# First layer of a three-layer block: new column order, convolution, normalisation and attention run beside later columns

## The chip, the cores and the metric

The kernel runs on one core of a Trainium2 chip, in one launch. The metric is the device time of that launch in microseconds, from first to last instruction with what lies around them. Five engines matter: TensorE (PE in the profile; its weight loads are listed apart as PEld), VectorE (DVE), ScalarE (ACT), GpSimd (POOL) and SyncE (SP), which issues nearly all DMAs. PSUM has eight banks of 512 fp32 columns: four are `lin_ps`, four are `ps`.

## The reference

256 tokens with 2048 features pass through three layers. Only the first is rebuilt:

```python
z = rmsnorm(x) @ w_in                                  # [256, 2048] @ [2048, 7168]
a_val, a_gt, a_gate, q, k, v, b_gate = split(z, 7 x 1024)
u  = (a_val + b0) * sigmoid(a_gt + b1)
y  = causal_depthwise_conv(u, w_dw, 31 taps) + b_dw    # per channel, along the tokens
y  = silu(layernorm(y) * ln_g + ln_b)                  # over the 1024 channels
ya = (y @ w_pw + b_pw) * silu(a_gate)
yb = causal_attention(q, k, v, 8 heads of 128) * silu(b_gate)
x  = x + concat(ya, yb) @ w_out
```

With 256 tokens the block-sparse attention of the reference is plain causal attention. The second layer is a latent attention with an indexer, the third a gated DeltaNet with a Fourier branch and an MLP of 8192; each ends with a projection that is added to `x`.

## The kernel before

**Products in two parts.** Every fp32 weight is split on the chip: ACT rounds a tile to fp32r (`w_hi`, helper `hi`), POOL subtracts (`w_lo`, L543), and the activations are kept as such a pair as well (`a` and `b`, `[P, 16, 2, 256]`, feature chunks by high or low part by tokens). Weights come in *units* of 128x1024 (512 KB, one DMA), through four slots of `raw`, `w_hi` and `w_lo`. The order of the units is fixed by hand (`LINEARS`), and each engine counts them: `raw_in`, `hi_done`, `lo_done`, `unit_used`. ACT may split unit u once unit u - 4 is used up. In the text, unit numbers are those of this order: 0 to 111 are `w_in`, 112 to 119 the pointwise matrix `w_pw`, 120 to 151 `w_out`.

**Two kinds of units.** A *product* unit (`product`) has weights stationary, 4 chunks of features and 256 output columns. For each chunk and each of two column halves it issues one matmul of 512 columns (the high weights on both parts of the activations, L1889) and one of 256 (the low weights on the high part, L1891): 8 pairs. Four units make a *group*, whose result has features on partitions; one DVE reduction adds its two parts and moves it into `z` (`group_free` counts these evictions, L1130, L1175, L1199). A *wide* unit (`outer_unit`, L1929 to L1931) has activations stationary and 512 output columns moving: 12 matmuls of 512, with tokens on partitions in the result. `w_out` uses wide units. A group may start when the group two before it is evicted.

**The first layer, in order.** TensorE runs groups 0 to 23 in a row, in the order of the columns of `w_in`. ACT takes the sigmoid of two channel chunks at a time (L694), and DVE runs the convolution in four rounds of two chunks, 58 tap instructions each (L1202), beside groups 8 to 23. Then come, on TensorE:

1. the channel sum over partitions with a matrix of ones (L1947), group 24, and the sum of squares in the same way (L1953);
2. groups 25 to 27, during which DVE and ACT finish the normalisation in the layout with features on partitions;
3. the eight units of `w_pw`; after each group DVE adds the parts (L1240), the bias and the gate (L1244), and splits the result (L1248, L1250);
4. the attention, in a loop of four rounds of two heads with nothing else between its steps: transpose of v (L1967), scores (L1970), mask, maximum, exp, scale, transposes of the probabilities (L1977), product with v (L1982), gate and split (L1284, L1286);
5. `w_out` (32 wide units).

The second layer's attention has rounds of two heads too, but with product units between the steps: scores (L2129), some units, transposes (L2137), some units, product with v (L2146), with ACT's exp at L811 and its scaling at L817. Most of its rounds have the causal upper part left out: 128 + 256 columns of scores instead of 2 x 256.

Of the kernel before, what the change touches and what calls it, by code (L numbers as in the profile page):

```python
# [17 lines left out]
F32 = mybir.dt.float32  # L18
# [7 lines left out]
P = 128  # L26
# [58 lines left out]
GROUPS = (("even_w_in", 28), ("even_w_pw", 4), ("even_w_out", 4), ("odd", 38), ("odd_w_out", 4), ("w_in_2", 20),  # L85
# [79 lines left out]
for _ph in range(4):  # L165
    OUTS[f"mlp{_ph}"] = (UNIT0["mlp"] + 64 * _ph + 32, GROUP0["mlp"] + 12 * _ph + 8)
PLAIN = ("even_w_out", "w_o_2", "mlp0", "mlp1", "mlp2")
# [6 lines left out]
def build(nc, t, out):  # L174
    ctx = ExitStack()
    with ctx:
# [11 lines left out]
        def rounds(name, names):  # L188
# [81 lines left out]
        ln_act = steps("ln_act", [f"sq{s}" for s in range(4)] + ["root"] + [y for s in range(4) for y in (f"silu{s}a", f"silu{s}b")]  # L270
                       + [f"hi{s}" for s in range(4)] + ["agate", "bgate"])
        ln_pe = steps("ln_pe", ["mean"] + [f"var{s}" for s in range(4)])
        ln_dve = steps("ln_dve", [f"c{s}" for s in range(4)] + ["rstd"] + [f"n{s}" for s in range(4)] + [f"lo{s}" for s in range(4)])

        at_pe = [steps(f"at_pe{w}", ["vt", "s", "pt", "o"]) for w in range(2)]
        at_dve = [rounds(f"at_dve{w}", ["vtok", "mask", "max", "neg", "rsum", "n0", "n1", "ptc", "o", "hi", "lo"]) for w in range(2)]
        at_act = [steps(f"at_act{w}", ["qs", "vs", "p0", "p1"]) for w in range(2)]
        pw_dve = steps("pw_dve", ["g0", "g1", "hi", "lo"])
# [44 lines left out]
        e_q, e_v, e_vt = ([z[:, 8 * w + n, :] for w in range(2)] for n in range(3))  # L323
        e_s, e_pt = ([z[:, 8 * w + n:8 * w + n + 2, :] for w in range(2)] for n in (3, 5))
# [12 lines left out]
        addm = dmask[:].rearrange("p a b -> p (a b)")[:, 0:3 * P]  # L337
        o_flat = [v.rearrange("p a b -> p (a b)") for v in o_s]
# [69 lines left out]
        def _(sp):  # L408
# [24 lines left out]
            def stream_out(name, u0, row0=0):  # L433

                v = t[name].rearrange("(k p) n -> p k n", p=P)
                with sp.Fori(0, NB) as i:
                    col = sp.snap(i * BLK)
                    for j in range(8):
                        slot = (u0 + j) % SLOTS
                        sp.wait_ge(lo_done, i * 8 + (u0 + j - SLOTS + 1))  # L440
                        sp.dma_start(raw[:, slot].rearrange("p (k n) -> p k n", k=2),
                                     v[:, row0 + 2 * j:row0 + 2 * j + 2, bass.ds(col, BLK)]).then_inc(raw_in[slot], 16)
# [9 lines left out]
            for q in range(4):  # L452
                load(4 + q, q, first[:, q * UK:(q + 1) * UK, UN:2 * UN])
# [6 lines left out]
            stream("even_w_in", 8, 26, 4, col0=2 * UN)  # L460
# [7 lines left out]

            def free_slot(u):
                sp.wait_ge(lo_done, u - SLOTS + 1)  # L470
                return u % SLOTS
# [87 lines left out]
        def _(act):  # L559
# [122 lines left out]
            his(8, 24)  # L682

            with act.Fori(0, 4) as i:
                for n in range(16):
                    slot = n % SLOTS
                    act.wait_ge(raw_in[slot], i * 64 + 16 * ((32 + n) // SLOTS + 1))
                    act.wait_ge(unit_used, i * 16 + (32 + n - SLOTS + 1))
                    nc.scalar.activation(w_hi[:, slot], raw[:, slot], ACT.Copy).then_inc(hi_done, 1)  # L689
                    if n == 3:  # L690
                        act.wait_ge(group_free, 8)
                        for y in range(2):
# [3 lines left out]
            for n in range(4):  # L696
                hi(96 + n, n)
# [1743 lines left out]
```

## Time and profile before

| | us |
|---|---|
| median of 3 runs | 2332.21 |
| lowest, highest | 2326.82, 2333.15 |
| the profiled execution | 2328.57 |
| its span, first to last instruction | 2326.8 |
| PE busy | 2245.7 (97%) |
| POOL busy | 1727.3 (74%) |
| DVE busy | 1025.9 (44%) |
| ACT busy | 1049.6 (45%) |

Times inside the execution count from the start of its span. A PE matmul's own duration is longer than the distance to the next, because they are pipelined: the pace is read from the distances of starts, or from a stretch divided by its count. "PEclk" is the granted clock of TensorE as a share of full speed.

### The profile page before, as it was taken

What the parts mean: (1) busy time and instruction counts of PE and PEld (TensorE: products, weight loads), DVE (VectorE), ACT (ScalarE), POOL (GpSimd) and SP (SyncE); (2) the same over time, 40 slices, a digit from 0 to 9 for tenths busy, and PEclk for the clock granted to TensorE, in tenths of its full rate; (3) what the DMA queues carried; (4) which work ended last, traced back from release to release, by engine and by line L of the source; (5) the groups of instructions that cost most, each with busy time, mean ns of one, the idle gap of its engine ahead of it and who ended that gap; (6) DMA issues with size and microseconds to landing.
All of it is one profiled execution on the core that took longest, in us unless ns stands there. A gap on an engine that the chain in (4) does not pass through costs nothing.

```text
span 2326.8 us, 35399 instructions
## 1 busy us (share of the span) xinstructions
PE 2245.7 (97%) x12194; PEld 1925.9 (83%) x12194; DVE 1025.9 (44%) x1798; ACT 1049.6 (45%) x1442; POOL 1727.3 (74%) x723
## 2 busy tenths in 40 slices
PE   7999996899999999999999999999999999999998
PEld 6888885778888778888888888887888888888886
DVE  2176647212765133365656553503831631731731
ACT  5444453345457554445353535445333333333343
POOL 6888873478756876565565657887888888888886
PEclk9999998899999999999999999999999999999999
DMA  6666652355545655454444534565666666666654
GB/s 212 189 190 189 189 156 80 98 183 148 162 127 154 215 163 154 127 154 114 140 130 125 145 109 162 183 212 157 190 190 191 188 190 192 187 189 191 188 189 146
DMA packets 325519, 383.86 MB, mean 165 GB/s; under 512 B 14654, under 2 KB 263333, under 8 KB 325157
## 3 DMA queue, kind: packets, MB, share of 16 engines
q1 hardware_dynamic: 321333, 376.75, 54.0%
q10 hardware_dynamic: 4080, 5.64, 0.8%
q8 instruction: 74, 1.21, 0.2%
q14 instruction: 32, 0.26, 0.0%
HBM read 380.24 MB, written 2.10 MB: 164 GB/s over the span
## 4 chain that ended last, share of the span: by engine, by line
PE 92%; DVE 3%; issue 1%; ACT 1%; POOL 1%; DMA 1%; ACTq 0%; DVEq 0%; POOLq 0%; SPq 0%
PE lin_ps L1889 37%; PE lin_ps L1891 18%; PE lin_ps L1929 8%; PE lin_ps L1931 8%; PE lin_ps L1930 8%; PE ps L2295 1%; PE ps L1860 1%; POOL w_lo L543 1%; PE ps L2288 1%; PE ps L2294 1%; PE ps L2214 1%; DVE scr L1244 1%; DMA raw<-in_odd_w_out 0%; PE ps L2146 0%; PE lin_ps L2008 0%
## 5 line engine op out<-in xcount | busy, mean ns | idle before, releaser
L543 POOL TENSOR_TENSOR w_lo<-raw,w_hi 128x1024 fp32r<-128x1024 f32 x716 | 1726.9, 2421 | 580.8 <-ACT w_hi L571 450.5
L1889 PE MATMUL lin_ps<-a,w_hi 128*128 128x512 f32 x3328 | 1184.1, 400 | 0.4 <-POOL w_lo L543 0.4
L1891 PE MATMUL lin_ps<-a,w_lo 128*128 128x256 f32 x3328 | 929.5, 279 | 0.0
L1889 PEld LDWEIGHTS lin_ps<-a,w_hi 128*128 128x128 f32 x3328 | 626.0, 188 | 149.7 <-issue 2.9
L1891 PEld LDWEIGHTS lin_ps<-a,w_lo 128*128 128x128 f32 x3328 | 628.1, 189 | 2.6 <-issue 1.9
L571 ACT ACTIVATE w_hi<-raw 128x1024 fp32r<-128x1024 f32 x360 | 378.8, 1060 | 452.4 <-PE lin_ps L1891 257.2
L582 ACT ACTIVATE w_hi<-raw 128x1024 fp32r<-128x1024 f32 x260 | 276.3, 1063 | 442.4 <-PE lin_ps L1891 283.2
L1929 PE MATMUL lin_ps<-w_hi,b 128*128 128x512 f32 x768 | 300.1, 391 | 2.1 <-POOL w_lo L543 1.9
L1931 PE MATMUL lin_ps<-w_hi,b 128*128 128x512 f32 x768 | 298.8, 389 | 0.0
L1930 PE MATMUL lin_ps<-w_lo,b 128*128 128x512 f32 x768 | 298.8, 389 | 0.0
L1929 PEld LDWEIGHTS lin_ps<-w_hi,b 128*128 128x128 f32 x768 | 144.3, 188 | 33.4 <-POOL w_lo L543 3.5
L1931 PEld LDWEIGHTS lin_ps<-w_hi,b 128*128 128x128 f32 x768 | 144.2, 188 | 30.0
L1930 PEld LDWEIGHTS lin_ps<-w_lo,b 128*128 128x128 f32 x768 | 144.3, 188 | 29.8
L1889 PE MATMUL lin_ps<-b,w_hi 128*128 128x512 f32 x416 | 147.8, 399 | 5.8 <-DVE scr L1240 3.1
L1147 DVE SCALAR_TENSOR_TENSOR x<-x,lin_ps 128x512 f32<-128x512 f32 x32 | 20.6, 684 | 297.2 <-PE lin_ps L1931 297.2
L1891 PE MATMUL lin_ps<-b,w_lo 128*128 128x256 f32 x416 | 116.5, 280 | 0.0
L689 ACT ACTIVATE w_hi<-raw 128x1024 fp32r<-128x1024 f32 x64 | 67.9, 1061 | 95.3 <-PE lin_ps L1891 95.3
L1889 PEld LDWEIGHTS lin_ps<-b,w_hi 128*128 128x128 f32 x416 | 78.1, 188 | 26.3 <-DVE scr L1240 3.4
L1202 DVE SCALAR_TENSOR_TENSOR ps<-z,vec,ps 128x254 f32<-128x254 f32 (+28 forms) x232 | 88.9, 466 | 0.1
L1821 DVE TENSOR_REDUCE scr<-lin_ps 128x512 f32<-128x1024 f32 x32 | 39.2, 1225 | 112.4 <-PE lin_ps L1891 112.4
L1823 DVE SCALAR_TENSOR_TENSOR scr<-scr 128x512 f32<-128x512 f32 x32 | 86.5, 2704 | 1.1
L1825 DVE CAST b<-scr 128x512 f32 x32 | 78.8, 2464 | 5.1 <-DVE scr L1823 5.1
(379 smaller groups left out, 2135.5 us busy)
## 6 DMA issues: line engine op xcount, KB each, us to landing
raw<-in_w_in SPq DMA_DIRECT2D x144, 512.0 KB, 3.7
raw<-in_w_mlp_up SPq DMA_DIRECT2D x128, 512.0 KB, 3.8
raw<-in_w_mlp_down SPq DMA_DIRECT2D x128, 512.0 KB, 4.7
raw<-in_even_w_in SPq DMA_DIRECT2D x112, 512.0 KB, 3.6
raw<-in_odd_w_in SPq DMA_DIRECT2D x40, 512.0 KB, 3.7
raw<-in_even_w_out SPq DMA_DIRECT2D x32, 512.0 KB, 3.6
raw<-in_odd_w_out SPq DMA_DIRECT2D x32, 512.0 KB, 4.6
raw<-in_w_o SPq DMA_DIRECT2D x32, 512.0 KB, 4.8
```

Of the source, the lines that this page charges most:

```text
L543: nc.gpsimd.tensor_tensor(w_lo[:, slot], raw[:, slot], w_hi[:, slot].bitcast(F32), ALU.subtract).then_inc(lo_done, 1)
L571: nc.scalar.activation(w_hi[:, slot], raw[:, slot], ACT.Copy).then_inc(hi_done, 1)
L582: nc.scalar.activation(w_hi[:, slot], raw[:, slot], ACT.Copy).then_inc(hi_done, 1)
L689: nc.scalar.activation(w_hi[:, slot], raw[:, slot], ACT.Copy).then_inc(hi_done, 1)
L1202: nc.vector.scalar_tensor_tensor(out=acc[c][:, :, k:T], in0=u[c][:, :, 0:T - k], scalar=per_channel(w + 8 * (TAPS - 1 - k) + c), in1=acc[c ...
L1823: nc.vector.scalar_tensor_tensor(out=tm2, in0=tmp, scalar=0.0, in1=tmp, op0=ALU.max, op1=ALU.mult).then_inc(ml_dve.sem, 1)
L1825: nc.vector.tensor_copy(bb[:, :, 0, :], tm2).then_inc(ml_dve.sem, 1)
L1889: nc.tensor.matmul(acc, hi[:, k, m * P:(m + 1) * P], src[:, kk].rearrange("p s n -> p (s n)"), start=(q == 0 and k == 0), stop=False)
L1891: last = nc.tensor.matmul(acc[:, 0:T], lo[:, k, m * P:(m + 1) * P], src[:, kk, 0, :], start=False, stop=(q == n - 1 and k == UK - 1))
L1929: nc.tensor.matmul(acc, ah, hi[:, k, :], start=(kk == 0), stop=False)
L1930: nc.tensor.matmul(acc, ah, lo[:, k, :], start=False, stop=False)
L1931: last = nc.tensor.matmul(acc, al, hi[:, k, :], start=False, stop=(kk == DC - 1))
```

## The change

1. **Column order.** `w_in` is read as the list `EVEN` says: value and sigmoid gate of the convolution alternate (groups 0 to 7), then q, k (8 to 15), v (two wide groups, 16 and 17), the attention's gate (18 to 21), the convolution's gate (22 to 25). 28 groups become 26; the number of units stays 112.
2. **Convolution.** Its four rounds are unrolled and start once their own two groups are there; the evictions of groups 2 to 11 are placed between the taps.
3. **Values.** v is computed with tokens on partitions (wide units), so no head's v is transposed.
4. **Normalisation.** The convolution's result is turned onto tokens (16 transposes of 128x128), DVE takes mean and variance with `bn_stats` and `bn_aggr`, scales, and 16 transposes turn it back between wide units 4 and 5 of group 17. ACT applies silu in PSUM. The products with ones are gone.
5. **Attention.** Its four rounds run between units 96 and 115: scores before unit 96, 101, 106, 111, transposes two units later, product with v four units later. The upper triangle is left out as in the second layer; ACT scales the probabilities and rounds the output.
6. **Pointwise units.** For each weight half three matmuls of 256 columns (high-high, high-low, low-high) into the same columns, so no reduction follows; the bias and gate are applied in PSUM, ACT rounds into `a`, DVE subtracts.
7. **`w_out`** starts with the attention's half (`FROM`), then takes the pointwise half from `a`. SP's loop for it and for the other wide projections is unrolled.
8. **All product units of the kernel:** `product` issues high, high, low, low instead of high, low, high, low.

```diff
+EVEN = []
+for _n in range(4):
+    EVEN += [(Z_AVAL + 2 * _n, _n * UN), (Z_AGT + 2 * _n, CW + _n * UN)]
+EVEN += [(Z_Q + 2 * _n, 3 * CW + _n * UN) for _n in range(4)]
+EVEN += [(Z_K + 2 * _n, 4 * CW + _n * UN) for _n in range(4)]
+EVEN += [(Z_V + 4 * _n, 5 * CW + _n * 512) for _n in range(2)]
+EVEN += [(Z_BGATE + 2 * _n, 6 * CW + _n * UN) for _n in range(4)]
+EVEN += [(Z_AGATE + 2 * _n, 2 * CW + _n * UN) for _n in range(4)]
+E_ROUNDS = (96, 101, 106, 111)
...
 # ScalarE
+            for last, i in ((11, 0), (22, 1), (31, 2), (42, 3)):
+                his_up(8 if i == 0 else (12, 23, 32)[i - 1], last)
+                gates(i)
+            his_up(43, 74)
+            preload(1)
+            his_up(75, 77)
+            act.wait_ge(ln_dve.sem, ln_dve.at("ag1"))
+            nc.scalar.activation(bn_root, ..., ACT.Sqrt, bias=eps[:, 0:1]).then_inc(ln_act.sem, 1)
+            his_up(78, 80)
+            act.wait_ge(ln_pe.sem, ln_pe.at("t2"))
+            for c in range(8):                     # silu in PSUM; unit 81 after the fourth
...
+            for r, first in enumerate(E_ROUNDS):
+                his_up(done_to + 1, first + 2)
+                if r == 0:
+                    act.wait_ge(group_free, 22)
+                    gate = z[:, Z_BGATE:Z_BGATE + 8, :]
+                    nc.scalar.activation(gate, gate, ACT.Silu).then_inc(ev_act.sem, 1)
...                                                # exp, scale, two units, (r == 3: silu of a_gate), one unit
 # VectorE
+            taken = ({12: 2, 24: 3}, {5: 4, 17: 5, 28: 6}, {8: 7, 20: 8, 30: 9}, {10: 10, 22: 11})
...
+            for g in range(12, 17):
+                even_out(g)
...                                                # bn_stats x4, bn_aggr x2, reciprocal, scale x4, masks
+            for r in range(4):
+                both(e_scores, r)
+                if r == 3:
+                    even_out(25)
+                both(e_sums, r)
+                both(e_turned, r)
+                if r in (1, 2):
+                    even_out(22 + r)
+                if r == 3:
+                    pw_gate(0)
+                both(e_out, r)
...
 # TensorE, product
                     for m in range(2):
-                        acc = lin_ps[:, 2 * parity + m, :]
-                        nc.tensor.matmul(acc, hi[:, k, m * P:(m + 1) * P], src[:, kk].rearrange("p s n -> p (s n)"),
-                                         start=(q == 0 and k == 0), stop=False)
-                        last = nc.tensor.matmul(acc[:, 0:T], lo[:, k, m * P:(m + 1) * P], src[:, kk, 0, :],
+                        nc.tensor.matmul(lin_ps[:, 2 * parity + m, :], hi[:, k, m * P:(m + 1) * P],
+                                         src[:, kk].rearrange("p s n -> p (s n)"), start=(q == 0 and k == 0), stop=False)
+                    for m in range(2):
+                        last = nc.tensor.matmul(lin_ps[:, 2 * parity + m, 0:T], lo[:, k, m * P:(m + 1) * P], src[:, kk, 0, :],
                                                 start=False, stop=(q == n - 1 and k == UK - 1))
 # TensorE, first layer
+            for g in range(16):
+                for q in range(4):
+                    product(4 * g + q, g, g % 2, q, 4, q, a, 0, in_ready if g == 0 else None, g >= 2)
+            for j in range(8):
+                wide_unit(E_VAL + j, 16, j, of_a, j)
...                                                # 16 transposes
+            for j in range(8):
+                if j == 5:
+                    pe.wait_ge(ln_dve.sem, ln_dve.at("n11"))
...                                                # 16 transposes back
+                wide_unit(E_VAL + 8 + j, 17, j, of_a, j)
...
+            for u in range(E_REST, PW + 8):
+                for r, first in enumerate(E_ROUNDS):
+                    if u == first:
+                        e_scores(r)
+                    if u == first + 2:
+                        e_turned(r)
+                    if u == first + 4:
+                        e_outputs(r)
+                if u < PW:
+                    g = 18 + (u - E_REST) // 4
+                    product(u, g, g % 2, u % 4, 4, u % 4, a, 0, None, True)
+                else:
+                    pw_unit(*divmod(u - PW, 2))
```

## Rows read from the trace of the kernel before

**Rows 1.** The page: busy time of the engines, and its two costliest groups.

```profile
PE 2245.7 (97%) x12194; PEld 1925.9 (83%) x12194; DVE 1025.9 (44%) x1798; ACT 1049.6 (45%) x1442; POOL 1727.3 (74%) x723
...
L543 POOL TENSOR_TENSOR w_lo<-raw,w_hi 128x1024 fp32r<-128x1024 f32 x716 | 1726.9, 2421 | 580.8 <-ACT w_hi L571 450.5
L1889 PE MATMUL lin_ps<-a,w_hi 128*128 128x512 f32 x3328 | 1184.1, 400 | 0.4 <-POOL w_lo L543 0.4
```

**Rows 2.** Windows of the first layer: stretch, its length, busy time per engine, clock, DMA.

```profile
28.70:289.60 260.90, 260.90 (x1508) 228.20 (x1506) 125.50 (x285) 114.62 (x114) 227.05 (x95) 1.00 0.63 191
289.60:308.60 19.00, 18.32 (x98) 15.38 (x96) 7.16 (x12) 8.68 (x10) 12.75 (x6) 1.00 0.50 152
...
358.80:370.90 12.10, 5.82 (x32) 4.84 (x32) 11.66 (x10) 5.20 (x7) 8.13 (x4) 0.99 0.44 139
370.90:428.70 57.80, 36.28 (x113) 26.82 (x114) 38.80 (x92) 18.66 (x51) 0.37 (x1) 0.65 0.05 15
428.70:515.90 87.20, 87.17 (x385) 71.83 (x383) 6.23 (x11) 36.63 (x43) 73.36 (x31) 1.00 0.57 176
```

**Rows 3.** Waits of PE from 358 to 428.7: total, times, longest.

```profile
PE ps L1977 <- DVE z L1270: 13.1, 4, 5.4
PE ps L1967 <- ACT z L740: 11.1, 4, 3.2
PE lin_ps L1889 <- DVE scr L1240: 3.1, 1, 3.1
```

**Rows 4.** Lines of PE, 28.7 to 289.4: count, busy time, mean ns.

```profile
L1889 PE MATMUL lin_ps<-a,w_hi 128*128 128x512 f32 x752 | 260.8, 394 | 0.0
```

**Rows 5.** The same for a stretch of the MLP, 2138.2 to 2222.

```profile
L1889 PE MATMUL lin_ps<-a,w_hi 128*128 128x512 f32 x238 | 84.1, 399 | 0.0
```

**Rows 6.** Timelines: start, length, instruction. A pair and the next, then eight small matmuls.

```profile
150.11 0.39 PE L1889 MATMUL lin_ps<-a,w_hi 128*128 128x512 f32 x1
150.34 0.27 PE L1891 MATMUL lin_ps<-a,w_lo 128*128 128x256 f32 x1
150.46 0.40 PE L1889 MATMUL lin_ps<-a,w_hi 128*128 128x512 f32 x1
...
1049.78 1.06 PE L2295 MATMUL ps<-z 128*128 128x128 f32 x8
```

**Rows 7.** Timeline of TensorE in one attention round of the second layer.

```profile
720.55 1.47 PE L2129 MATMUL ps<-z 128*128 128x128 f32 x8
721.67 0.58 PE L1889 MATMUL lin_ps<-a,w_hi 128*128 128x512 f32 x1
...
727.50 0.82 PE L2137 MATMUL ps<-ident,z 128*128 128x128 f32 x6
728.08 0.48 PE L1889 MATMUL lin_ps<-a,w_hi 128*128 128x512 f32 x1
...
730.94 1.47 PE L2146 MATMUL ps<-z 128*128 128x256 f32 x8
732.17 0.47 PE L1889 MATMUL lin_ps<-a,w_hi 128*128 128x512 f32 x1
```

**Rows 8.** DVE and ACT in that round.

```profile
720.75 1.23 DVE L1296 TENSOR_REDUCE z<-lin_ps 128x512 f32<-128x1024 f32 x1 [1.47 <-PE lin_ps L1891]
...
723.39 0.41 ACT L811 ACTIVATE z<-z,stat 128x128 f32<-128x128 f32 x1 [3.63 <-DVE stat L1434]
...
725.68 1.49 ACT L817 ACTIVATE z<-z,stat 128x128 f32<-128x128 f32 x4
```

**Rows 9.** Lines of DVE in one convolution round, 160.3 to 204.6.

```profile
L1202 DVE SCALAR_TENSOR_TENSOR ps<-z,vec,ps 128x254 f32<-128x254 f32 (+28 forms) x58 | 22.2, 467 | 0.0
```

**Rows 10.** Lines of ACT, 305 to 357.

```profile
L731 ACT ACTIVATE z<-z 128x2048 f32<-128x2048 f32 x1 | 1.9, 1902 | 0.0
L709 ACT ACT_TABLE_LOAD x1 | 1.3, 1283 | 0.0
```

**Rows 11.** Lines of DVE, 505 to 600: nearest to the new scaling from PSUM.

```profile
L1334 DVE TENSOR_SCALAR scr<-lin_ps,stat 128x512 f32<-128x512 f32 x2 | 1.4, 746 | 0.0
```

More of the change, by code:

```diff
@@ L727, in _, with his_up @@
-            for n in range(4):
-                hi(108 + n, n)
-            his(UNIT0["even_w_pw"], 8)
-            act.wait_ge(group_free, 28)
-            nc.scalar.activation(z[:, Z_BGATE:Z_BGATE + 8, :], z[:, Z_BGATE:Z_BGATE + 8, :],
-                                 ACT.Silu).then_inc(ln_act.sem, 1)
-            ahead(UNIT0["even_w_out"])
-            act.wait_ge(ln_dve.sem, ln_dve.at("lo3"))
-            with act.Fori(0, HE // 2) as i:
+            def his_up(first, last):
+                for u in range(first, last + 1):
+                    hi(u, u % SLOTS)
@@ new lines, in _, with pointwise @@
+                his_up(first + 5, first + 5)
+                done_to = first + 5
+                def pointwise(g):
+                    bank = 2 * ((PW_G + g) % 2)
+                    act.wait_ge(pw_dve.sem, pw_dve.at("g1", g))
+                    nc.scalar.activation(a[:, 2 * g:2 * g + 2, 0, :], lin_ps[:, bank:bank + 2, 0:T], ACT.Copy).then_inc(pw_act.sem, 1)
+                if r == 3:
+                    pointwise(0)
+                for w in range(2):
+                    act.wait_ge(at_dve[w].sem, at_dve[w].at("gate", r))
+                    nc.scalar.activation(b[:, 8 + 2 * r + w, 0, :], ps[:, 2 * w, 0:T], ACT.Copy).then_inc(at_act[w].sem, 1)
@@ L1225, in _ @@
-            even_out(25)
+            for g in range(12, 17):
+                even_out(g)
+            for q in range(TT):
+                for h in range(2):
+                    dve.wait_ge(ln_pe.sem, ln_pe.at("t1"))
+                    nc.vector.bn_stats(bn[:, 12 * q + 6 * h:12 * q + 6 * h + 6], ps[:, 2 * q + h, :]).then_inc(ln_dve.sem, 1)
+            for q in range(TT):
+                dve.wait_ge(ln_dve.sem, ln_dve.at(f"bn{q}1"))
+                nc.vector.bn_aggr(bn_two[:, 2 * q:2 * q + 2], bn[:, 12 * q:12 * q + 12]).then_inc(ln_dve.sem, 1)
@@ L1287, in _ @@
+            for g in range(1, 4):
+                pw_gate(g)
+                pw_low(g)
             to_x("even_w_out", 1)
@@ L1942, in _ @@
             vectors(0, 1, 2)
[L1943 removed]
+            in_ready = normed(0)
             pe.wait_ge(bld, 3)
[L1945 to L1955 removed]
@@ new lines, in pw_unit @@
+            def pw_unit(g, q):
+                u, bank = PW + 2 * g + q, 2 * ((PW_G + g) % 2)
+                if q == 0:
+                    pe.wait_ge(group_free, PW_G + g - 1)
+                pe.wait_ge(lo_done, u + 1)
+                hi = w_hi[:, u % SLOTS].rearrange("p (k n) -> p k n", k=UK)
+                lo = w_lo[:, u % SLOTS].rearrange("p (k n) -> p k n", k=UK)
+                for k in range(UK):
+                    kk = UK * q + k
+                    for m in range(2):
+                        acc, cols = lin_ps[:, bank + m, 0:T], slice(m * P, (m + 1) * P)
+                        nc.tensor.matmul(acc, hi[:, k, cols], b[:, kk, 0, :], start=(kk == 0), stop=False)
+                        nc.tensor.matmul(acc, hi[:, k, cols], b[:, kk, 1, :], start=False, stop=False)
+                        last = nc.tensor.matmul(acc, lo[:, k, cols], b[:, kk, 0, :], start=False, stop=(kk == 2 * UK - 1))
+                last.then_inc(unit_used, 1)
```

438 lines of the change are left out of this document (211 added, 227 removed).

## Prediction, made before the changed kernel was run

> **What bounds the kernel now.** I read the page first: PE is busy 2245.7 us of the span, POOL 1727.3 us [rows 1]. PE sets the time nearly everywhere, and POOL is next: a unit costs it 2.42 us, while PE takes 8 pairs of matmuls for one. So any gain must come from PE: idle time, extra instructions, or its pace.
>
> The windows of the first layer come second [rows 2]. From 28.7 to 289.6 PE is full: 752 pairs in 260.8 us [rows 4], 0.347 us each, 2.77 us a unit. The wide units of `w_out` go at 87.2 us / 385 = 0.2265 us a matmul, 2.72 us a unit [rows 2]. Between them lie 139 us that look different. From 370.9 to 428.7 stands the attention alone: 57.8 us, PE busy 36.3, POOL 0.4, and the granted clock at 0.65 on average, that is, much of it at the 1.2 GHz level, after idle gaps [rows 2].
>
> The waits name the gaps: 13.1 us for the scaled probabilities, 11.1 us for the copies of v, 3.1 us for the pointwise stage's split [rows 3]. DVE, ACT and POOL do nothing for other work meanwhile. The question is what is left of these 139 us when the attention lies between product units.
>
> **What goes away.**
> - Windows 289.6 to 308.6: 19.0 us hold one group (32 x 0.347 = 11.1); the rest, 7.9 us, is the two products with ones and one wait for the convolution [rows 2, 4].
> - 358.8 to 370.9: 12.1 us hold two pointwise units (5.5); 6.6 us are waits for the pointwise results [rows 2].
> - 370.9 to 428.7: all 57.8 us [rows 2].
> Together 72.3 us.
>
> **What comes.**
> - Attention beside units. The second layer's round has the same shapes. Its scores hold PE from 720.55 to 721.67, its transposes from 727.50 to 728.08, its outputs from 730.94 to 732.17: 1.12 + 0.58 + 1.23 = 2.93 us [rows 7]. Four rounds: 11.7 us.
> - 32 transposes of 128x128. Eight fp32 matmuls of that size take 1.06 us from first start to last end, 0.78 without the last one's length, 0.11 each [rows 6]: 3.6 us.
> - v as two wide groups: 16 x 2.72 instead of 16 x 2.77: -0.8 us.
> - Pointwise units: 24 matmuls of 256 columns instead of 8 pairs. A pair costs 0.347 and a wide matmul 0.2265 [rows 2, 4], so the 256 columns cost 0.120; 24 x 0.120 = 2.88 instead of 2.77, eight times: +0.9 us.
>
> **What the cover leaves open.** Between scores and transposes two units run. In the second layer that was just enough: ACT's last scaling ended at 725.68 + 1.49 = 727.17, and PE came to it at 727.50 [rows 7, 8], although an eviction of 1.23 us stood before DVE's mask [rows 8]. The rounds of the new code are the same, with more room later (two units before the outputs), but two are not:
> - Round 0: ACT must first wait for the eviction of group 21, then take silu of the whole `b_gate` (1.9 us) and load the table for exp (1.28 us) [rows 10]. The eviction ends 1.3 us after the scores begin; silu ends at 3.2, the table is there at 4.5. The second layer's exp started 2.84 us after its scores [rows 7, 8]. So everything is 1.7 us later, 0.33 of which was spare: I take a stall of 1.5 us, with 0 and 3 as the ends.
> - Round 3: `even_out(25)` stands before the sums on DVE; unit 111 ends 1.12 + 2.77 = 3.9 us after the scores begin, its eviction at 5.1, the scalings near 6.8 where PE arrives at 6.7. Taken at 0.2 us. Behind it, silu of `a_gate` needs 3.2 us on ACT and delays `pw_gate(0)`; by my count the first pointwise group is out about a microsecond before its bank is wanted, so nothing more.
> By the Trainium skill, page "ScalarE: Activation LUTs", section "What ACT_TABLE_LOAD costs", a table switch costs about 1.28 us and a drain of 1.38 us behind it; by that the stall of round 0 would be 2.9 us. The trace has 1.283 us for the load [rows 10] and shows no drain row; I use the rows.
>
> **The convolution and the normalisation.** The 752 pairs from 28.7 on are 94 units, so two of the 96 were done before [rows 4]: group g ends at 34 + 11.1 g, group 1 at 45, group 15 at 201. A convolution round needs 22.2 us of taps [rows 9] and some 3 us of small instructions, with three evictions of 1.23 us 29 us; four in a row from 49 us (eviction of group 1, table 1.28, two sigmoids) are done near 165, with waits for group 9 in round 2. Each eviction placed between taps comes within some 3 us of its group's end, against 11 us of room. This work is hidden by 64 product units; were DVE late by a group, PE would stand still.
>
> For the normalisation DVE gets the turned data near 224.5, after group 16 (21.8 us). Eviction, four `bn_stats`, two `bn_aggr` and four scalings follow. No row has a `bn_stats` of 512; a scaling of 512 from PSUM took 0.75 us [rows 11]; I take 0.75 for both (bounds 0.25 to 1.5). Between them ACT's square root waits behind the split of unit 77, which needs unit 73 used: 231. So the scalings end near 235, and PE asks at 224.5 + 5 x 2.72 = 238.1. The cover is 3 us; with 1.5 us an instruction, PE would wait 0 to 3 us. I take 0. Back-transposes, silu and split then have the rest of group 17 and 32 units before they are needed.
>
> **The new order inside `product`** touches 460 units, 3680 pairs, so 0.01 us on each pair would be 37 us. It counts most after the attention. Now the 512 takes 0.23 to the next start and the 256 takes 0.12 [rows 6], each with one weight load. The new order has the same four matmuls and loads, but two loads behind 256 columns follow each other. Eight weight changes in a row at 0.11 us [rows 6] say the loads keep up, and the wide units say that a repeated bank costs nothing. The pace is not always the same: in the MLP 238 pairs take 84.1 us, 0.353 each [rows 5], against 0.347 [rows 4]. Whether the new order settles at the one or the other no row says. I take 0; between the two paces the bound is 3680 x 0.006 = 22 us either way, and both ends are less than that, since some stretches already have each.
>
> **Sum.** 72.3 - 11.7 - 3.6 + 0.8 - 0.9 - 1.5 - 0.2 = 55.2 us. The profiled execution took 2328.6 (span 2326.8): 2273.4. It stands 3.6 us below the median of the runs, by which it would be 2277. I say 2275.
>
> **Rivals.**
> - *The cover does not hold.* Each round keeps part of its old waits: chains through DVE and ACT are long, and splits of units queue on ACT between exp and scaling. If half of the 24.2 us of the two big waits [rows 3] stay, and some clock is lost with them, the gain is 35 to 43 us: 2285 to 2297. Against it: rows 7 and 8, the same chain with the same cover.
> - *The pace improves.* If all product matmuls went at the pace of rows 4: 3328 of them fill 1184.1 us [rows 1], 0.356 each, but that holds starts after waits too. That is 0.009 x 3680 = 33 us at the very most; where only stretches at the 0.353 of rows 5 gain, 10 to 15: 2262.
> - *The other side: two 256s in a row wait for the whole weight load.* If a second load could begin only when the first is through and used, the gap between the two low matmuls would grow from 0.12 us. There are 1840 such places. It decides at 55 / 1840 = 0.030 us each; at 0.07 more the kernel is 74 us slower, 2402. Rows 6 speak against it: loads in fp32 keep 0.11.
>   The Trainium skill's "TensorE: Matmul & The Clock Gate", section "LDWEIGHTS (loading the stationary operand)", gives the columns over 1.2, an estimate of 107 ns for 128, which fits behind 256 columns; by it this rival falls.
> - *The change does not do what it says*: a new wait (ACT's split of units 81 to 83 behind eight silus, or POOL behind that) eats all. It would have to be 55 us, and the largest I can count is under 3.
>
> **Chances.** My forecast 0.60 (own range 2264 to 2284); cover fails 0.16; pace improves 0.14; second load or bad pace everywhere 0.08, of which 0.04 ends slower than before; other 0.02. I leave out the far tails: 2252 to 2296. A change of 0.3% is 7 us, about what this measurement can tell from none. Faster 0.94, within it 0.01, slower 0.05.
>
> **What the profile after would show.** `w_out` starts near 374 instead of 428.7. PE is full from 29 us on with clock 1.00; no stretch has POOL idle. Waits of PE on the attention under 3 us, the largest in round 0 on ACT's scaling. Convolution done before 170. Pairs at 0.347 to 0.353 in all later stages. I am wrong if the four starts inside `product` are not two at 0.23 and two at 0.12, if PE waits at `n11`, or if gaps follow the transposes in every round. Later layers should take the same time.

## The result, and the profile after

The changed kernel takes 2273.81 us (median of 4 runs, 2272.94 to 2274.89), the kernel before 2332.09 us in the same session (4 runs): the ratio is 0.9761, interval 0.9747 to 0.9774, so 58.3 us or 2.4% faster. The span of the profiled execution went from 2326.8 to 2273.1 us. The page of the changed kernel, beside [rows 1]:

```profile
PE 2217.1 (98%) x12170; PEld 1909.5 (84%) x12170; DVE 1027.0 (45%) x1762; ACT 1036.3 (46%) x1442; POOL 1715.4 (75%) x721
...
L582 POOL TENSOR_TENSOR w_lo<-raw,w_hi 128x1024 fp32r<-128x1024 f32 x716 | 1715.1, 2403 | 538.6 <-ACT w_hi L610 440.4
```

PE and POOL still lead in the same order. PE's busy time fell by 28.6 us, the span by 53.7: about half of what went was idle time. The windows of the first layer, in the columns of [rows 2]; the first ends where unit 63 is used, the second and third are values with normalisation and groups 18 to 21, the fourth and fifth the attention and the pointwise units, the last is `w_out`:

```profile
29.30:202.10 172.80, 172.80 (x995) 150.78 (x994) 119.26 (x283) 71.55 (x75) 149.56 (x63) 1.00 0.63 192
202.10:249.20 47.10, 47.10 (x226) 39.45 (x225) 10.67 (x17) 24.87 (x32) 38.19 (x17) 1.00 0.59 178
249.20:293.80 44.60, 44.60 (x258) 38.92 (x257) 7.29 (x8) 17.46 (x18) 38.57 (x17) 1.00 0.63 190
293.80:353.30 59.50, 57.91 (x333) 49.63 (x332) 28.48 (x50) 29.69 (x59) 36.52 (x16) 1.00 0.44 137
353.30:379.70 26.40, 25.59 (x208) 24.87 (x207) 9.82 (x21) 17.98 (x28) 19.39 (x9) 1.00 0.53 161
379.70:466.20 86.50, 86.50 (x384) 71.65 (x383) 6.66 (x11) 39.49 (x47) 76.96 (x33) 1.00 0.66 197
```

The stretch of 57.8 us at a clock of 0.65 [rows 2] is gone: PE is full up to 293.8 us, and the clock is 1.00 in every stretch. All waits that the view of waits lists for PE between 30 and 380 us (total, times, longest), against 27 us in [rows 3]:

```profile
PE ps L2057 <- ACT z L767: 0.9, 3, 0.5
PE lin_ps L1941 <- POOL w_lo L582: 0.4, 2, 0.3
PE lin_ps L2035 <- POOL w_lo L582: 0.2, 1, 0.2
```

Where the time went is read from the starts of the long stretches of wide units, which both kernels have. In us from the start of the span:

```
                 w_out    odd w_out   MLP 0     MLP 1     MLP 2     MLP 3     end
before           428.2    750.6       1696.1    1873.6    2051.1    2228.7    2326.8
changed          379.7    701.7       1645.9    1822.1    1998.3    2174.5    2273.1
earlier by        48.5     48.9         50.2      51.5      52.8      54.2      53.7
```

The first layer gave 48.5 us, and the later layers 5.2 more, 1.3 or 1.4 of it from one MLP start to the next. The prediction had 55 and nothing. The experiments look at both differences. From `w_out` to MLP 0 one execution differs from the next: in the kernels of the experiments that are alike there (e3 to e9, and e11) this stretch takes 1264.2 to 1267.0 us. So the 1.7 us that the changed kernel gained there are not clear of noise; the steps from one MLP to the next are.

The first is in the attention's rounds. TensorE's small matmuls in rounds 0 and 1 (timeline; a bracket is PE's idle time before the line):

```profile
293.78 1.47 PE L2049 MATMUL ps<-z 128*128 128x128 f32 x8
...
301.08 1.24 PE L2057 MATMUL ps<-ident,z 128*128 128x128 f32 x6 [0.25 <-ACT z L767]
...
308.11 1.47 PE L2065 MATMUL ps<-z 128*128 128x256 f32 x8
...
312.21 1.47 PE L2049 MATMUL ps<-z 128*128 128x128 f32 x8
...
319.48 1.24 PE L2057 MATMUL ps<-ident,z 128*128 128x128 f32 x6 [0.23 <-ACT z L767]
...
326.65 1.47 PE L2065 MATMUL ps<-z 128*128 128x256 f32 x8
```

A round is five units and 2.93 us of attention, 5 x 2.774 + 2.93 = 16.80 us. From scores to scores they took 18.43, 18.54 and 18.41 us. DVE in round 1, and what GpSimd and ACT did meanwhile:

```profile
313.65 0.69 DVE L1283 TENSOR_REDUCE stat<-z 128x2 f32<-128x512 f32 x1
314.38 1.96 DVE L1285 TENSOR_SCALAR stat<-stat 128x2 f32<-128x2 f32 x1
316.25 0.54 DVE L1280 SCALAR_TENSOR_TENSOR z<-ps,dmask 128x384 f32<-128x384 f32 x1
316.83 0.69 DVE L1283 TENSOR_REDUCE stat<-z 128x2 f32<-128x512 f32 x1
317.55 0.17 DVE L1285 TENSOR_SCALAR stat<-stat 128x2 f32<-128x2 f32 x1
```

```profile
311.57 4.74 POOL L582 TENSOR_TENSOR w_lo<-raw,w_hi 128x1024 fp32r<-128x1024 f32 x2 [1.73 <-ACT w_hi L610]
...
316.37 0.41 ACT L762 ACTIVATE z<-z,stat 128x128 f32<-128x128 f32 x1 [4.01 <-DVE stat L1285]
...
318.64 1.48 ACT L767 ACTIVATE z<-z,stat 128x128 f32<-128x128 f32 x4
```

The same instruction, L1285, takes 0.17 us for one head and 1.96 us for the other. It negates two numbers per partition. The long one ends at 316.34, when GpSimd's second subtraction ends (311.57 + 4.74 = 316.31). The exp starts behind it, and the scaling, the splits queued behind it on ACT, and GpSimd's subtractions come later. Of the 1.8 us that it is too long, 1.2 to 1.3 reach the round (e3 below); the rest was spare time in the chain. The second head's negation starts at 317.55, when GpSimd stands idle, and is short.

Round 0 shows no long negation: its two start at 296.43 and 297.82 and take 0.17 us each, and GpSimd has nothing to do from 294.84 to 302.75. It shows the silu and the table load on ACT instead, as the prediction had it:

```profile
295.24 1.92 ACT L758 ACTIVATE z<-z 128x2048 f32<-128x2048 f32 x1 [2.92 <-DVE z L1209]
297.17 1.28 ACT L762 ACT_TABLE_LOAD   x1
298.47 0.40 ACT L762 ACTIVATE z<-z,stat 128x128 f32<-128x128 f32 x1
```

```profile
292.47 2.37 POOL L582 TENSOR_TENSOR w_lo<-raw,w_hi 128x1024 fp32r<-128x1024 f32 x1 [0.39 <-ACT w_hi L610]
302.75 2.41 POOL L582 TENSOR_TENSOR w_lo<-raw,w_hi 128x1024 fp32r<-128x1024 f32 x1 [7.91 <-ACT w_hi L610]
```

### The profile page after: what moved, and what is told of

It is laid out like the page before. It is cut to its first block, busy times and chain, and to the rows that moved or that the text cites. A ratio compares the mean times of both kernels' runs of the same rounds, so it can differ in the third digit from the quotient of the medians.

```text
span 2273.1 us, 33387 instructions
## 1 busy us (share of the span) xinstructions
PE 2217.1 (98%) x12170; PEld 1909.5 (84%) x12170; DVE 1027.0 (45%) x1762; ACT 1036.3 (46%) x1442; POOL 1715.4 (75%) x721
## 4 chain that ended last, share of the span: by engine, by line
PE 92%; DVE 2%; issue 2%; ACT 2%; POOL 1%; DMA 1%; ACTq 0%; POOLq 0%; DVEq 0%
PE lin_ps L1941 35%; PE lin_ps L1944 17%; PE lin_ps L1982 9%; PE lin_ps L1980 9%; PE lin_ps L1981 9%; POOL w_lo L582 1%; PE ps L2392 1%; PE ps L1913 1%; PE ps L2385 1%; PE ps L2391 1%; PE ps L2311 1%; ACT w_hi L610 1%; PE ps L2243 0%; DMA raw<-in_odd_w_out 0%; PE lin_ps L2166 0%
## 5 line engine op out<-in xcount | busy, mean ns | idle before, releaser
L1941 PE MATMUL lin_ps<-a,w_hi 128*128 128x512 f32 x3200 | 1020.9, 400 | 0.9 <-POOL w_lo L582 0.8
L1944 PEld LDWEIGHTS lin_ps<-a,w_lo 128*128 128x128 f32 x3200 | 601.9, 188 | 142.2
L1944 PE MATMUL lin_ps<-a,w_lo 128*128 128x256 f32 x3200 | 629.9, 278 | 0.0
L1941 PEld LDWEIGHTS lin_ps<-a,w_hi 128*128 128x128 f32 x3200 | 491.4, 189 | 8.5 <-issue 5.2
L1980 PE MATMUL lin_ps<-w_hi,b 128*128 128x512 f32 x704 | 274.7, 390 | 1.6 <-POOL w_lo L582 1.5
L1981 PE MATMUL lin_ps<-w_lo,b 128*128 128x512 f32 x704 | 274.0, 389 | 0.0
L1982 PE MATMUL lin_ps<-w_hi,b 128*128 128x512 f32 x704 | 273.9, 389 | 0.0
L1941 PE MATMUL lin_ps<-b,w_hi 128*128 128x512 f32 x352 | 112.5, 401 | 2.9 <-POOL w_lo L582 2.2
L1980 PE MATMUL lin_ps<-w_hi,a 128*128 128x512 f32 x256 | 99.8, 390 | 0.0
L1982 PE MATMUL lin_ps<-w_hi,a 128*128 128x512 f32 x256 | 99.6, 389 | 0.0
L1981 PE MATMUL lin_ps<-w_lo,a 128*128 128x512 f32 x256 | 99.6, 389 | 0.0
L1880 DVE TENSOR_TENSOR b<-scr,b 128x512 f32 x32 | 92.4, 2889 | 4.7 <-DVE b L1878 0.5
```

What stands on the lines that cost most here:

```text
L1880: nc.vector.tensor_tensor(bb[:, :, 1, :], tm2, bb[:, :, 0, :].bitcast(F32), ALU.subtract).then_inc(ml_dve.sem, 1)
L1941: nc.tensor.matmul(lin_ps[:, 2 * parity + m, :], hi[:, k, m * P:(m + 1) * P], src[:, kk].rearrange("p s n -> p (s n)"), start=(q == 0 and ...
L1944: last = nc.tensor.matmul(lin_ps[:, 2 * parity + m, 0:T], lo[:, k, m * P:(m + 1) * P], src[:, kk, 0, :], start=False, stop=(q == n - 1 and ...
L1980: nc.tensor.matmul(acc, ah, hi[:, k, :], start=(j == 0 and k == 0), stop=False)
L1981: nc.tensor.matmul(acc, ah, lo[:, k, :], start=False, stop=False)
L1982: last = nc.tensor.matmul(acc, al, hi[:, k, :], start=False, stop=(j == 7 and k == 1))
```

## The experiments

Eleven kernels ran. Ratios are against the kernel before on the same chip. The changed kernel itself wasn't run again beside them, so "slower" or "faster than the changed kernel" compares two medians of different sessions; by the intervals of the ratios such a difference is good to 4 or 5 us, and a smaller one has to be read from the traces. "A chunk" below is two matmuls of 512 and two of 256 columns, and its time the mean sum of the four distances of starts, those over 0.76 us left out.

The traces allow a closer comparison. From the first matmul of v to the first of `w_out`, neither the start-up nor the later layers count. That stretch holds the values, groups 18 to 25, the attention and the pointwise units:

```
us                       v starts   w_out starts   between   rounds 0, 1, 2
changed                  202.1      379.7          177.61    18.43 18.54 18.41
e1, the old order again  200.6      378.9          178.27    18.44 18.60 18.41
e3, no negation          200.6      374.6          174.01    18.43 17.22 17.23
e4, silu later           201.0      377.4          176.41    17.22 18.54 18.41
e5, no cover             200.6      405.1          204.49
e6, both                 200.9      373.7          172.81    17.23 17.23 17.22
e7, low ones crossed     201.3      378.9          177.60    18.42 18.56 18.39
e8, e6 and a reduction   200.5      373.3          172.79    17.22 17.23 17.23
e9, e6 and a scalar form 200.5      377.0          176.41    17.22 18.55 18.41
e10, four and four       201.8      375.0          173.17    17.26 17.24 17.24
e11, e6 once more        200.5      373.3          172.81    17.23 17.22 17.23
```

### What is the new order inside `product` worth?

`e1_old_order` is the changed kernel with the old order:

```diff
-  for m: matmul(512, hi)          # high, high
-  for m: matmul(256, lo)          # low, low
+  for m: matmul(512, hi); matmul(256, lo)
```

> The changed kernel with the matmuls inside product in their former order (high, low, high, low). Theory (the order gave the 5 us that the later layers are shorter): slower than the changed kernel by 4 to 8 us, about 2279; stages of product pairs fall back to two paces, 1387 ns for four pairs (0.347 each) in some and 1413 ns in others, instead of 1393 ns everywhere. Rival (the order does nothing, the pace comes from where the loops start after the new first layer): within 1 us of the changed kernel, one pace.

Measured: 2280.46 us (5 runs, 2278.54 to 2281.69), ratio 0.9788 (0.9773 to 0.9803): 6.6 us slower than the changed kernel, as the theory of the order had it; its rival, no difference and one pace, falls.

`e2_new_order_alone` is the kernel before with the new order and nothing else of the change.

> The kernel before with only the order high, high, low, low inside product. Theory (order): faster than before by 4 to 8 us, about 2326, and 1393 ns for four pairs in every stage, so the MLP's stretches shorter and the first layer's 96 units longer by 0.6 us. Rival (the order does nothing): 2332, within 1 us.

Measured: 2321.6 us (6 runs), ratio 0.9965 (0.9951 to 0.9979): 8.2 us of gain against the median of all its runs of the kernel before (2329.78), where 4 to 8 were expected. So the order is worth 6 to 8 us, from either side. The profiled executions differ by 6.5 us (2326.8 and 2320.3), and `w_out` starts at 427.3 against 428.2 us, so most of it lies in the later layers: their 1898.6 us became 2320.3 - 427.3 = 1893.0, and with the old order in the changed kernel they are 2278.7 - 378.9 = 1899.8, against 1893.4 with the new.

`e7_crossed_order` asks whether the bank matters. In the old order each low matmul used the bank of the high one just before it, in the new order neither does. With `for m in (1, 0)` in the second loop the first low matmul does again, the second one does not (the expectation says each, which is more than the edit does).

> The changed kernel with high 0, high 1, low 1, low 0 inside product, so that each low matmul goes to the bank of the matmul just before it, as in the former order, while the two of 256 columns still stand together. If the pace hangs on the sequence of sizes (512, 512, 256, 256), it is that of the changed kernel, 697 ns for a chunk, and the time within 1 us. If it hangs on banks that repeat, there are two paces again or a third, and the time moves by 3 us or more.

Measured: 2272.77 us (4 runs), 0.9757 (0.9739 to 0.9774), that is no difference (-1.0 us by the medians, 0.01 us in the stretch above). What the chunks cost:

```
us a chunk                       groups 0 to 15, MLP 0 MLP 1 to 3    mean of all
before (512 256 512 256)         0.6933                0.7066        0.7002
changed (512 512 256 256)        0.6967                0.6967        0.6967
e1, the old order again          0.6933                0.7066        0.7014
e2, the new order alone          0.6967                0.6967        0.6967
e7, low ones crossed             0.6967                0.6966        0.6968
```

The two paces of [rows 4] and [rows 5] belong to the old order. The new one has a single pace between them: it loses 0.003 us a chunk where the old one was at the better level and gains 0.010 where it was at the worse. Where the old pace changes is not tied to the place in the kernel: the kernel before runs the whole first layer at 0.6933, e1 only its groups 0 to 15, and its groups behind the values at 0.703 to 0.707. A stretch of the MLP shows the difference by the count alone (lines of PE, 1912 to 1996 us, first the changed kernel, then e1; 84 us / 242 and / 238 is 0.347 and 0.353 us a pair, where a count is good to one pair; by the distances it is 0.348 and 0.353):

```profile
L1941 PE MATMUL lin_ps<-a,w_hi 128*128 128x512 f32 x242 | 76.0, 395 | 0.0
```

```profile
L1942 PE MATMUL lin_ps<-a,w_hi 128*128 128x512 f32 x238 | 84.1, 399 | 0.0
```

The busy times of these two must not be compared: with two high matmuls side by side their overlap counts once.

### Does the negation wait for GpSimd, and what does it cost?

`e3_no_negation` scales the scores by the negative factor, takes the minimum, and lets exp run with a scale of -1. The small instruction is gone, and exp gives the same values:

```diff
-  stt(z, ps, DH ** -0.5, addm, mult, add);  tensor_reduce(max) -> stat[0:2]
-  wait;  tensor_scalar(stat[2:4], stat[0:2], -1.0, mult)
+  stt(z, ps, -(DH ** -0.5), addm, mult, subtract);  tensor_reduce(min) -> stat[2:4]
```

> The changed kernel, but the first layer's attention computes the negated scores, so that a minimum gives the bias of exp and the small negation on DVE (128x2) is gone. Theory (in rounds 1 to 3 the first of these waits until GpSimd's running subtraction ends, 1.9 us instead of 0.17, and the whole chain to the scaled probabilities is late by that): scores to transposes 6.7 us instead of 7.3 in rounds 1 and 2, unit 104's and 109's low weights no longer late, 2 to 4 us off the time: about 2271. Rival (the chain is late because of ACT's own queue): only the instruction's own 0.17 us is gained, the wait before the transposes stays, 0 to 0.5 us.

Measured: 2269.42 us (5 runs, 2267.83 to 2271.33), 0.9745 (0.973 to 0.976), 4.4 us faster than the changed kernel by the medians, and 177.61 - 174.01 = 3.6 us in the stretch from v to `w_out`. Rounds 1 and 2 take 17.22 and 17.23 us instead of 18.54 and 18.41; round 0 is still at 18.43. From scores to transposes round 1 takes 6.89 us instead of 7.27 (6.7 was expected). The rival, a chain late by ACT's own queue, would have left all but 0.5 us, and falls.

`e4_silu_later` leaves the negation and moves the silu of `b_gate`, which only the last step of the round needs, behind the round's scalings and two splits:

```diff
-  if r == 0: wait group_free 22; Silu(b_gate)      # before exp
   exp, scale, split first + 3, first + 4
+  if r == 0: wait group_free 22; Silu(b_gate)
```

> The changed kernel with silu of b_gate behind exp, scaling and two splits of round 0 instead of before them. Theory (round 0 is late because silu of 1.9 us and the table of exp stand before it): the 0.3 us wait before round 0's transposes and most of its second head's wait go, 0.5 to 1.5 us off the time. Rival (silu is hidden beside DVE's part of the chain): nothing, within 0.3 us.

Measured: 2271.94 us (5 runs, 2271.81 to 2273.37), 0.9754 (0.9739 to 0.9768), 1.9 us faster than the changed kernel, which medians of two sessions can't tell from none. The traces can: 177.61 - 176.41 = 1.2 us. Now round 0 takes 17.22, and rounds 1 and 2 18.54 and 18.41. The two causes are told apart round by round: each edit cures its own rounds and no other.

`e6_both_fixes` has both, and `e11_both_fixes_again` is the same kernel, run beside another for comparison.

> The changed kernel with the negation gone and silu of b_gate later, both. If the two waits are separate, as the theory has it, their gains add: 3 to 5 us off the changed kernel, about 2270, and PE without an idle stretch between unit 96 and w_out except round 3's. If the late splits on ACT are what PE waits for at unit 99, 104 and 109, 1 us stays of each round.

> e6_both_fixes once more, on the chip of e8 to e10, to stand beside them: 2266 to 2270, rounds of 17.2 us.

Measured: 2268.2 us (4 runs, 2267.32 to 2268.62), 0.9738 (0.9721 to 0.9756), and 2269.52 us (4 runs, 2267.59 to 2269.78), 0.974 (0.9719 to 0.9761): 4 to 6 us faster than the changed kernel, and 4.8 us in the stretch from v to `w_out`, the sum of e3's 3.6 and e4's 1.2. No kernel here is faster. The view of waits lists none for PE between 30 and 400 us, and all three rounds take 17.23 us:

```profile
292.58 1.47 PE L2047 MATMUL ps<-z 128*128 128x128 f32 x8
...
299.47 0.82 PE L2055 MATMUL ps<-ident,z 128*128 128x128 f32 x6
...
305.71 1.47 PE L2063 MATMUL ps<-z 128*128 128x256 f32 x8
...
309.81 1.47 PE L2047 MATMUL ps<-z 128*128 128x128 f32 x8
```

The last pair of questions: is it the small instruction as such, or its kind? Both kernels are e6 with one unneeded instruction of 128x2 put back between the minimum and exp. Only its kind differs:

```diff
   tensor_reduce(min) -> stat[2:4];  wait
+  e8:  tensor_reduce(stat[0:2], stat[2:4], max)        # over one element: a copy
+  e9:  tensor_scalar(stat[0:2], stat[2:4], 1.0, mult)  # a copy too
```

> The kernel of e6_both_fixes with a useless DVE instruction where the negation stood, in line between the minimum and exp: a copy of 128x2 made by a tensor_reduce. Both theories of the late negation: the instruction's own 0.2 us. If GpSimd holds back only certain forms of DVE instruction (theory), this one takes 0.2 us also while GpSimd subtracts, rounds stay at 17.2 us, and the time is that of e6 within 1 us. If any small instruction after a reduction is late (rival), it takes 1.9 us in rounds 1 to 3 and the time goes up by 3 to 4 us.

> As e8, but the useless copy of 128x2 is made by a tensor_scalar (times 1.0), the form of the negation. Theory: in rounds 1 to 3 the first of them lasts until GpSimd's subtraction ends (about 1.9 us), rounds 1 and 2 take 18.4 us again, and the time is 3 to 4 us above e6. Rival: as e8, no difference between the two forms.

Measured: e8 2268.39 us (4 runs, 2267.55 to 2268.79), 0.9736 (0.9716 to 0.9757); e9 2272.61 us (4 runs, 2271.92 to 2273.31), 0.9756 (0.9735 to 0.9777). The two differ by 4.2 us, 3.6 of it between v and `w_out`; rounds 1 and 2 are back at 18.55 and 18.41 us in e9 alone. So the rival that any small instruction there is late falls. GpSimd and DVE at the same place (timelines), in e8 and then in e9:

```profile
308.79 4.75 POOL L582 TENSOR_TENSOR w_lo<-raw,w_hi 128x1024 fp32r<-128x1024 f32 x2 [1.39 <-ACT w_hi L610]
...
311.59 0.15 DVE L1285 TENSOR_REDUCE stat<-stat 128x2 f32<-128x2 f32 x1
```

```profile
308.83 4.74 POOL L582 TENSOR_TENSOR w_lo<-raw,w_hi 128x1024 fp32r<-128x1024 f32 x2 [1.37 <-ACT w_hi L610]
...
311.63 1.96 DVE L1285 TENSOR_SCALAR stat<-stat 128x2 f32<-128x2 f32 x1
...
318.49 2.40 POOL L582 TENSOR_TENSOR w_lo<-raw,w_hi 128x1024 fp32r<-128x1024 f32 x1 [4.92 <-ACT w_hi L610]
```

Under the same subtractions the reduction takes 0.15 us and the scalar form ends with GpSimd's instruction (311.63 + 1.96 = 313.59, 308.83 + 4.74 = 313.57). Behind it GpSimd then stands for 4.92 us, because ACT splits late. The Trainium skill, page "SBUF — State Buffer", section "Who interferes with whom", says that DVE and GpSimd share one pair of ports which an instruction holds to its end, that `tensor_scalar` can ask for the pair and that `tensor_reduce` never does on this chip. The two runs agree with it, for an instruction of two numbers per partition; no run shows the ports themselves. Not every other small form waits, either: in e6 the reciprocal of 128x2 lies inside GpSimd's subtractions and takes 0.15 us.

```profile
309.17 4.74 POOL L582 TENSOR_TENSOR w_lo<-raw,w_hi 128x1024 fp32r<-128x1024 f32 x2 [1.79 <-ACT w_hi L610]
...
313.04 0.15 DVE L1287 RECIPROCAL stat<-stat 128x2 f32<-128x2 f32 x1
```

### What is the cover itself worth?

`e5_no_cover` is the changed kernel with all four attention rounds in a row before the first pointwise unit, with no units between their steps:

```diff
-  if u == first: e_scores(r); if u == first + 2: e_turned(r); if u == first + 4: e_outputs(r)
+  if u == PW: for r in range(4): e_scores(r); e_turned(r); e_outputs(r)
```

DVE evicts groups 22 to 25 first, and ACT runs the rounds after the split of unit 115.

> The changed kernel with its attention's four rounds in one piece before the first pointwise unit, nothing between scores, transposes and outputs; all else as changed. Theory (the gain is the cover): a round is then a bare chain of about 10 to 11 us with PE idle for most of it and the granted clock down, against some 4.6 us that a round costs beside units; slower than the changed kernel by 22 to 30 us, about 2299. Rival (the gain came mostly from the smaller work of a round: no transposed v, no upper triangle, scaling on ACT): slower by less than 12 us.

Measured: 2300.58 us (4 runs, 2299.57 to 2301.47), 0.988 (0.9862 to 0.9897), 26.8 us slower than the changed kernel, and 204.49 - 177.61 = 26.9 us in the stretch from v to `w_out`. The first three bare rounds take 13.56, 11.65 and 10.50 us (10 to 11 was expected). The rival, less than 12 us, falls. The window of the four rounds, and PE's waits between 30 and 400 us:

```profile
336.90:382.00 45.10, 24.35 (x90) 17.77 (x89) 22.85 (x54) 20.16 (x59) 3.43 (x2) 0.70 0.10 33
```

```profile
PE ps L2042 <- ACT z L767: 18.2, 4, 6.8
PE ps L2034 <- DVE b L1296: 2.5, 3, 0.8
```

The clock is 0.70 on average, near the 0.65 of [rows 2] and again between the levels of 1.2 and 2.4 GHz, and PE works for 24.35 of 45.1 us. The bare attention took 57.8 us before and 45.1 here: 12.7 us were gained without any cover. What can have gained them is that v needs no transposes, that the upper triangle is left out, and that ACT and not DVE scales the probabilities; no run separates these.

### More high matmuls together?

`e10_four_and_four` is e6 with the matmuls of two chunks taken together: four high, then four low.

> The kernel of e6_both_fixes with four high matmuls, then four low ones, for two chunks at a time. If each change from 512 to 256 columns costs the 3.4 ns by which a chunk is above 693.3 (two wide matmuls of 226.7 and two of 120), a chunk comes down to 695, 3 us for the whole kernel: 2265. If the pace hangs on how many of 256 stand together, it goes up above 697, or two paces return.

Measured: 2273.29 us (4 runs, 2271.94 to 2276.23), 0.9763 (0.9741 to 0.9785), some 4 us slower than e11 beside it. The theory that more of one kind in a row is better falls: a chunk costs 0.7000 us in groups 0 to 15 and 0.7017 in the MLP, against 0.6967 in e11 in both. The other half of the expectation came, a pace above 0.697, and with it two paces again. The timeline shows two chunks from 149.98 to 151.38, 1.40 us; its hundredths don't tell which of the eight matmuls is late:

```profile
149.98 1.09 PE L1941 MATMUL lin_ps<-a,w_hi 128*128 128x512 f32 x4
150.91 0.64 PE L1945 MATMUL lin_ps<-a,w_lo 128*128 128x256 f32 x4
151.38 0.39 PE L1941 MATMUL lin_ps<-a,w_hi 128*128 128x512 f32 x1
```

## Why the prediction was right, step by step

**The time.** 2275 was said, 2273.81 measured. The sum had 55.2 us against the profiled execution; the spans differ by 53.7. That closeness is partly luck: the first layer gave 6.7 less than the sum, and the later layers 5.2 more. Without the new order, which the sum had at nothing, the time is 2280.46 (e1).

**The cover.** The step that carries the prediction holds, in kind and nearly in size: 57.8 us out, the four rounds between units in. The sum makes of it 57.8 - 11.7 - 1.7 = 44.4 us. By e5 it was 12.7 + 26.8 = 39.5 us. PE's waits in the rounds are 0.9 us on ACT's scaling, where under 3 were said, but this did not bound the loss: the view counts a wait from the end of the matmul before, which lies behind the next start. By the starts, round 1 loses 1.31 us against e6: 0.38 before the transposes, 0.43 between the transposes of its two heads, and 0.50 in the two units behind them, of which the second waits for its low weights. Gaps like these, 0.3 to 0.5 us each, stand at the transposes in every round. The prediction had named gaps in every round as a sign that it was wrong; they came, and were small. It also had no stretch with POOL idle, and POOL is idle for 7.9 us in round 0 and 4.9 to 5.2 in each of the others.

**The rounds, the mis-sized term.** 16.80 us a round, with 1.5 more for the first and 0.2 for the last, became 18.43, 18.54 and 18.41, and what follows the fourth scores takes 30.5 us. Three parts:
- The silu and the table load in round 0 cost 18.43 - 17.22 = 1.2 us (e4) against 1.5. This mechanism was right, place and size.
- The negation costs 1.3 and 1.2 us in rounds 1 and 2 (e3) and about 1.1 in the last (30.5 us, and 373.7 - 344.3 = 29.4 in e6), 3.6 us together, which is also what e3 gives from v to `w_out`. The prediction had 0.2 for round 3 and nothing for the others. It took the chain's length from one round of the second layer, [rows 8], and what a small DVE instruction costs beside GpSimd it did not ask.
- A round without either still takes 17.23, 0.43 more. The prediction ended each segment at the start of the first product matmul behind it, and the first chunk from there is itself longer: in e6 0.89 us behind the scores (293.70 to 294.59), 0.78 behind the transposes and 0.79 behind the outputs, instead of 0.697, 0.37 us together. The rest is the pace of the new order. With the pointwise units of the last round this is some 2 us.

**The rest of the first layer.** The new order is at 0.3484 us a pair here, where the old had 0.347: 80 units before the first scores, 640 pairs, 1 us. Together 3.6 - 0.2 - 0.3 + 2 + 1 = 6.1 of the 6.7 us. Most of the remainder is the start-up, which differs between executions: the matmul at 28.70 in the profiled execution before (the start of the first stretch in [rows 2]) stands at 29.24 in the changed one, 0.5 us later, and v starts at 202.1 us there and between 200.5 and 201.3 in e3 to e9 and e11, which have the same pace up to it.

**Removed and added around it.** What neither the order (7.4 us, the middle of e1 and e2) nor the cover (26.8) nor the cheaper rounds (12.7) explain of 58.3 is 11.4 us. The sum had 7.9 + 6.6 + 0.8 - 0.9 - 3.6 = 10.8 for the products with ones, the pointwise waits, v and the transposes. No run took these terms one by one, and a remainder of four differences is itself uncertain by several us, so that the two agree shows little.

**Convolution and normalisation.** The taps end at about 165 us, said: near 165. The scalings of the normalisation end at 235.8, said: 235. PE comes to their result at 239.25, said: 238.1. So the cover was 3.5 us and PE did not wait (DVE, then PE):

```profile
225.83 2.49 DVE L1251 BATCH_NORM_STATS2 stat<-ps 128x6 f32<-128x512 f32 x4 [0.52 <-PE ps L2011]
228.24 0.32 DVE L1254 BATCH_NORM_AGGREGATE stat<-stat 128x2 f32<-128x12 f32 x2
232.62 0.17 DVE L1256 RECIPROCAL stat<-stat 128x2 f32<-128x2 f32 x1 [4.06 <-ACT stat L739]
232.82 2.96 DVE L1260 TENSOR_SCALAR scr<-ps,stat 128x512 f32<-128x512 f32 x4
...
239.25 1.91 PE L2019 MATMUL ps<-ident,scr 128*128 128x128 f32 x16
```

Four statistics take 2.49 us, four scalings 2.96, both near the 0.75 us each that was taken from [rows 11]. The 4.06 us of idle DVE are the square root queued behind ACT's split of unit 77, as worked out. The sixteen transposes take 1.67 us from their start at 223.88 to the next matmul of a wide unit at 225.55, 0.10 each.

**The order inside `product`.** It was taken at 0, with 22 us as the bound either way; it is 6 to 8 us. (The 460 units behind that bound are 444: the profile of the changed kernel has 3200 + 352 = 3552 pairs. Nothing hangs on it.) The step that failed is "settles at the one or the other": it is at neither. The later layers were said to take the same time and are 5.2 us shorter. The starts inside `product` are two at 0.23 and two at 0.12, as said.

**The rivals.** "The cover does not hold" (2285 and up) fell: the waits are 1.5 us in all. "The pace improves" was a real mechanism, and little more than half its size (6 to 8 us for 10 to 15): the worst stretches gained, as it said, while the good ones lost a little. "Two 256s in a row wait for a load" fell: two low matmuls and the distance to the next high one come to 0.23 to 0.24 us, the same as before. A new wait did appear, but it is worth 4 us and not 55.

**The table load.** The row decides between 1.28 us and 1.28 with a drain of 1.38 (the Trainium skill, "ScalarE: Activation LUTs", section "What ACT_TABLE_LOAD costs"): the load starts at 297.17 and the exp at 298.47, 0.02 us behind its end. No drain is to be seen, and the stall that silu and load make together is 1.2 us and not 2.9. In e6, where no silu stands before the exp, the load starts at 291.13, before the scores, and the exp waits for DVE until 295.23: the load lies in ACT's idle time and costs nothing, although it belongs to the exp.

**What stays open.** Why the old order has two paces, with 256 columns between the 512s each time, and why twos cost less than fours, no run here tells. The e7 run excludes only that the repeated bank of one low matmul in two matters. That the slower pace is a matter of where the weights lie in the four slots was not tried.

## What to carry to other kernels

When serial work is moved between matmuls, count every instruction of its chain, the smallest too, on an engine that shares something with a busy one: here two numbers per partition cost 1.1 to 1.3 us in each of three rounds, as much as a whole silu with its table load in the fourth, and writing the same algebra without the instruction gave 3.6 us back. An instruction that only the last step of a stage needs doesn't belong in front of its first. And when an edit changes the order of matmuls in a loop that runs for 444 units, measure it alone: between 0.003 us lost and 0.010 gained on a chunk came 6 to 8 us, as much as the first layer fell short of its sum.

## What the runs showed of the hardware that was not expected

- A `tensor_scalar` of 128x2 in fp32 from SBUF to SBUF takes 0.17 us alone and 1.96 us beside a GpSimd subtraction of 2.4 us, whose end it shares. Where GpSimd is idle (round 0, and the second head of round 1) it takes 0.17 us in the same kernel. A `tensor_reduce` of the same size in the same place takes 0.15 us (e8), and so does a reciprocal beside a subtraction (e6).
- The pace of a fixed set of matmuls (two of 512 columns, two of 256, one weight load each) depends on their order: 0.693 or 0.707 us alternating, 0.697 in twos, 0.700 or 0.702 in fours. The alternating order keeps one of its two paces through a long stretch of product units (groups 0 to 15, each MLP); in the layers between the two are mixed.
- A bare attention with 24 us of work in 45 us had a granted clock of 0.70 (e5), and the eight score matmuls of its second round took 2.93 us there; between product units the clock was 1.00 and they took 1.47.
- A table load did not wait for what its activation waited for: in e6 it ran from 291.13 and its exp started at 295.23.
